# Query heads prepared inside the first projection, keys and the rest left to the heads stage

## The chip, the core and the metric

The kernel runs on one core of a Trainium2 chip. The metric is the device time of one launch in microseconds (us). The engines are named as in the profile: PE (TensorE), DVE (VectorE), ACT (ScalarE), POOL (GpSimd), and SP, whose queue issues most transfers.

## What is computed

A two-layer model over 2048 latent and 256 context tokens (2304 in all, 18 tiles of 128), width 1024. Only the first half of layer 0 matters here:

```
h  = layer_norm(x) * (1 + scale) + shift          # scale, shift = silu(c) @ ada_w + ada_b
q, ga, k, v, u, gb = split(h @ w_in)               # q: 12 heads of 64; k, v: 4 heads; u: 4 groups of 64
q  = rope(rms_norm(q, q_gain));  k = rope(rms_norm(k, k_gain))
y  = [attention(q, k, v) * silu(ga), fourier(rms_norm(u, f_gain)) * silu(gb)] @ w_out
```

Layer 1 (an mLSTM mixer) and the rest of layer 0 are the same in both kernels. float32 products are made of three passes over parts: every operand is split into a high part and the rest (low part), and `split_mm` issues high x high, high x low and low x high.

## The kernel before

The program is a row of stages with a barrier between them: `modulation`, `projections` (layer 0), `heads`, attention, and so on. Engines meet only by semaphores; each engine runs its own instructions in the order written.

**projections(0)** computes proj0 = h @ w0, 2560 columns in NCH = 5 chunks of 512, token tile after token tile: 90 steps k = (c, t), 24 matmuls each. During chunk 0 each tile is also normalised and transposed (8 PE transposes through the PSUM tile `tp`). Step k needs the high and low parts of its tile, made by ACT (`high`, L374) and DVE (`low`, L479) into a ring of RING = 4 slots, two steps ahead from chunk 1 on. The result lands in one of NACC = 3 accumulators; ACT empties it in chunks 0, 3 and 4 (L398), DVE in chunks 1 and 2 (L490), into a ring of three stages that SP stores to DRAM (L329). So step k waits for the eviction of step k-3, and slot reuse makes `high(k+2)` wait for an older step. The weights of the next chunk come in two pieces of 1 MB: ACT loads and rounds them (L358), POOL subtracts (`low_w`, L433).

**heads** then reads proj0 back, tile by tile (ring of four tiles, 1536 columns each). ACT squares 20 groups of 64 (12 query heads, 4 key heads, 4 Fourier groups) with 20 instructions (L684); POOL makes the rotation table (L719) and the inverse norms (L728, L730, a power over 20 values); DVE multiplies by the table (L764), adds the halves (L772, L773), scales (L781 queries, L782 keys, L790 Fourier rows); PE transposes six pairs of query heads (L830) and four of keys (L837); ACT copies the high parts out (L693, L695), DVE the low parts (L798, L800). SP stores the queries of a tile with four transfers of 192 KB made of 512-byte pieces (L640). Keys stay in SBUF in `kres`. In the same stage run the `hm_` steps, the modulation vectors of the later stages: 16 pieces of `ada_w`, 1 MB each, one per tile, in nbuf = 2 buffers. At n == 4, SP also fills a constant part of `kres` (eight transfers, L665) and loads all values into `vres` (L666).

Of the kernel before, what the change touches and what calls it, by code (L numbers as in the profile page):

```python
# [20 lines left out]
F32 = mybir.dt.float32  # L21
# [5 lines left out]
P = 128  # L27
# [4 lines left out]
NT = T // P  # L32
# [206 lines left out]

def projections(nc, m, a, s, keep, layer):  # L240
# [11 lines left out]
    K, RING, NST, NACC, PIECES, NX = len(steps), 4, 3, 3, 2, 3  # L252
# [20 lines left out]
    if not L0:  # L273
# [6 lines left out]
        sg_done, sgz_done = m.sem(tag + "sg_done"), m.sem(tag + "sgz_done")  # L280
    x_ld, stats_done, var_done, rstd_done, xn_done = m.sem(tag + "x_ld", NX), m.sem(tag + "stats_d"), m.sem(tag + "var"), m.sem(tag + "rstd_d"), m.sem(tag + "xn")
# [21 lines left out]
    with nc.Block() as block:  # L303

        @block.sync
        def _(sp):
# [5 lines left out]
            for n in range(NX):  # L312
                load_x(n)
            for k, (c, t) in enumerate(steps):
# [22 lines left out]
        def _(act):  # L337
# [79 lines left out]
        def _(pool):  # L417
# [24 lines left out]
            for j in range(3, PIECES * NCH):  # L442
                low_w(j)

        @block.vector
        def _(dve):
# [50 lines left out]

            statistics(0)
# [23 lines left out]
        def _(pe):  # L522
# [72 lines left out]
def heads(nc, m, a, s, keep, kres, vres):  # L595

    NHD, NU, NR_RAW = NQ + NKV, FW // HD, 4
    NS, ND, NPAIR = NHD + NU, NQ + 2 * NKV, NQ // 2
    SPLIT = ((0, NQ), (NQ, NHD))
    raw = m.sb("hd_raw", [P, NR_RAW, C_GATE])  # L600
    rope = m.sb("hd_rope", [P, NR_RAW, 2, 32])
    table = m.sb("hd_table", [P, 2, 2, 4, 32])
# [1592 lines left out]
```

## Time and profile before

| what | value |
|---|---|
| median of 3 runs (lowest, highest) | 3894.47 us (3892.74, 3899.06) |
| profiled execution: its time, its span | 3897.25 us, 3895.6 us |
| busy share of the span: PE, DVE, ACT, POOL | 91%, 56%, 34%, 38% |
| projection 0, first x load to last step | about 38 to 580 us |
| heads stage, its first transfer to the first of the next stage | 583.88 to 761.28 us |
| mean granted PE clock, whole span | 0.942 |

The profile is one execution; the span is from the first to the last instruction. The two stages touched are 18% of it. PE is near full in the projection and about half idle in heads, so the shares of the whole span say little of either: each has to be read by itself.

### The profile page before, as it was taken

The page shows a single profiled execution, that of the slowest core. Times are in us where ns is not written, and L with a number is a line of the kernel's source. Part 1 is how long each engine was busy: PE and PEld are TensorE (multiplying, and loading weights), DVE is VectorE, ACT ScalarE, POOL GpSimd, SP SyncE. Part 2 cuts the span into 40 slices and gives each one's busy share as a digit, 9 for nine tenths or more (in the row PEclk, how much of TensorE's full clock was granted, in tenths as well). Part 3 has the DMA queues.
Part 4 walks back from the last instruction along what each step waited for, and adds up shares of the span by engine and source line. Part 5 has one row for each costly group of instructions (what it writes and reads, how often), then busy time and mean ns, then how long its engine had stood idle before and what let it go on. Part 6 is the DMA issues. An engine that isn't in the chain of part 4 may idle for free. (4 is left out here: it accounts for less than half of the span.)

```text
span 3895.6 us, 51321 instructions
## 1 busy us (share of the span) xinstructions
PE 3558.3 (91%) x17340; PEld 2683.5 (69%) x17340; DVE 2176.2 (56%) x3411; ACT 1315.6 (34%) x2466; POOL 1466.9 (38%) x937
## 2 busy tenths in 40 slices
PE   6999994689999999999959969999999995999798
PEld 4788872356666666666558857888998884887586
DVE  4633217856676666666536655333334443777576
ACT  2422326524444444444320034222223331664300
POOL 1100006627767776777713321000000101444354
PEclk8999995589999999999979979999999997999899
DMA  5321219811111111111065433212211112768553
GB/s 187 102 71 60 71 49 308 264 32 38 36 33 33 35 39 32 33 33 40 16 207 168 144 125 102 71 71 71 68 64 46 45 36 91 229 210 252 207 202 142
DMA packets 310817, 396.02 MB, mean 102 GB/s; under 512 B 79100, under 2 KB 207500, under 8 KB 310496
## 3 DMA queue, kind: packets, MB, share of 16 engines
q1 hardware_dynamic: 278304, 319.08, 26.2%
q10 hardware_dynamic: 21184, 37.46, 3.1%
q0 software_dynamic: 11136, 36.98, 2.4%
q8 instruction: 113, 1.85, 0.2%
q14 instruction: 80, 0.66, 0.1%
HBM read 269.76 MB, written 121.20 MB: 100 GB/s over the span
## 5 line engine op out<-in xcount | busy, mean ns | idle before, releaser
L1042 DVE TENSOR_REDUCE al_mx<-al_sx 128x1 f32<-128x512 f32 (+1 forms) x960 | 562.2, 631 | 268.9 <-PE al_sx L1119 255.4
L235 PE MATMUL pj_acc<-pj_whi,pj_h_hi 128*128 128x512 f32 x1808 | 709.9, 393 | 0.0
L236 PE MATMUL pj_acc<-pj_wlo,pj_h_hi 128*128 128x512 f32 x1808 | 706.0, 390 | 0.0
L237 PE MATMUL pj_acc<-pj_whi,pj_h_lo 128*128 128x512 f32 x1808 | 705.3, 390 | 0.0
L982 ACT ACTIVATE al_e<-al_st 128x1024 f32<-128x1024 f32 x432 | 442.6, 1025 | 578.1 <-PE al_st L1132 567.2
L479 DVE TENSOR_TENSOR pj_h_lo<-pj_hall,pj_h_hi 128x1024 fp32r<-128x1024 f32 x258 | 376.9, 1462 | 259.4 <-ACT pj_h_hi L374 259.3
L433 POOL TENSOR_TENSOR pj_wlo<-pj_wst,pj_whi 128x2048 fp32r<-128x2048 f32 x28 | 128.8, 4601 | 955.2 <-ACT pj_whi L358 955.2
L1012 POOL TENSOR_TENSOR al_acc_p<-al_acc_p,al_e 128x1024 f32<-128x1024 f32 x192 | 456.6, 2378 | 20.0 <-POOL al_acc_p L1012 0.4
L374 ACT ACTIVATE pj_h_hi<-pj_hall 128x1024 fp32r<-128x1024 f32 x258 | 270.8, 1056 | 530.8 <-PE pj_acc L237 513.4
L1141 PE MATMUL al_acc<-al_e,vres 128*64 128x512 f32 x1728 | 402.6, 601 | 0.0
L237 PEld LDWEIGHTS pj_acc<-pj_whi,pj_h_lo 128*128 128x128 f32 x1808 | 340.9, 189 | 71.9
L235 PEld LDWEIGHTS pj_acc<-pj_whi,pj_h_hi 128*128 128x128 f32 x1808 | 341.4, 189 | 70.4 <-issue 0.6
L236 PEld LDWEIGHTS pj_acc<-pj_wlo,pj_h_hi 128*128 128x128 f32 x1808 | 341.3, 189 | 69.5
L1131 PE MATMUL al_st<-al_qa,kres 128*128 128x512 f32 x864 | 344.9, 399 | 3.7 <-DMA al_qb<-al_negm 3.3
L1132 PE MATMUL al_st<-al_qb,kres 128*128 128x512 f32 x864 | 340.4, 394 | 0.0
L490 DVE COPY pj_stage<-pj_acc 128x512 f32<-128x512 f32 x122 | 84.3, 691 | 417.1 <-PE pj_acc L237 417.1
L1119 PE MATMUL al_sx<-kres,al_qx 128*128 128x512 f32 (+1 forms) x960 | 298.6, 394 | 9.6 <-DMA al_qx<-s_q 7.2
L1119 PEld LDWEIGHTS al_sx<-kres,al_qx 128*128 128x128 f32 x960 | 172.0, 191 | 158.6 <-issue 121.8
L1008 POOL TENSOR_TENSOR al_acc_p<-al_e 128x1024 f32<-128x1024 f32 x48 | 160.3, 3340 | 307.6 <-ACT al_e L982 307.6
L1141 PEld LDWEIGHTS al_acc<-al_e,vres 128*64 128x64 f32 x1728 | 111.2, 136 | 211.2 <-issue 194.8
L235 PE MATMUL mo_acc<-ow_whi,mo_y_hi 128*128 128x512 f32 x544 | 216.1, 397 | 0.0
L237 PE MATMUL mo_acc<-ow_whi,mo_y_lo 128*128 128x512 f32 x544 | 213.1, 392 | 0.0
(282 smaller groups left out, 5777.7 us busy)
## 6 DMA issues: line engine op xcount, KB each, us to landing
s_proj<-pj_stage SPq DMA_DIRECT2D x162, 256.0 KB, 2.0
pj_wst<-in_w ACTq DMA_DIRECT2D x28, 1024.0 KB, 5.7
ml_k<-s_proj SPq DMA_DIRECT2D x36, 512.0 KB, 4.4
ml_v<-s_proj SPq DMA_DIRECT2D x36, 512.0 KB, 8.7
mo_in<-s_proj SPq DMA_DIRECT2D x34, 512.0 KB, 6.0
hm_w<-in_ada_w SPq DMA_DIRECT2D x16, 1024.0 KB, 8.5
ml_qt<-s_qt SPq DMA_DIRECT2D x32, 512.0 KB, 6.1
s_h<-ml_h POOLq DMA_DIRECT2D x32, 512.0 KB, 8.0
```

The lines of the kernel that those rows point to most:

```text
L235: nc.tensor.matmul(out, s_hi, m_hi, start=start, stop=False)
L236: nc.tensor.matmul(out, s_hi, m_lo, start=False, stop=False)
L237: return nc.tensor.matmul(out, s_lo, m_hi, start=False, stop=stop)
L374: nc.scalar.activation(h_hi[:, k % RING], hall[:, :, t, :], ACT.Copy).then_inc(hi_done, 1)
L479: V.tensor_tensor(h_lo[:, k % RING], hall[:, :, t, :], h_hi[:, k % RING].bitcast(F32), ALU.subtract).then_inc(lo_done, 1)
L982: nc.scalar.activation(e[:, pair(p, j), :, :], st[(NP * p + j) % 2][:, :, 0:W], ACT.Exp).then_inc(e_done, 1)
L1012: nc.gpsimd.tensor_tensor(acc_p[:], acc_p[:], e[:, pair(p, j)], ALU.add).then_inc(add_p, 1)
L1042: V.tensor_reduce(mx[:, x:x + 1], slots[x % NSX][:, 0:spans[x % NS][1]], AX.X, ALU.max).then_inc(sx_max, 1)
L1119: mm(slots[x % NSX][:, 0:width], qx[:, p, i * P:(i + 1) * P], kres[:, g, lo:lo + width], start=True, stop=True).then_inc(sx_mm, 1)
L1131: mm(dst[:, t, 0:W], kres[:, g, keys], qa[:, p, :], start=True, stop=False)
L1132: y = mm(dst[:, t, 0:W], kres[:, NKV + g, keys], qb[:, p, :], start=False, stop=True)
L1141: y = mm(acc[t * HD:(t + 1) * HD, 0:W], vres[:, 2 * j + t, g, :], e[:, pair(p, j), t, :], start=(j == 0), stop=(j == NP - 1))
```

## The change

The twelve query heads leave `heads`. A new class `QueryHeads` does their work inside `projections(0)`, spread over the steps of chunks 1 to 4: tile n starts at step START + 3n = 21 + 3n, one tile every three steps. `due(k, after)` gives the tile whose piece with that offset falls on step k: SP reads 768 columns back at -2; ACT squares and POOL makes the table at -1; DVE sums and multiplies and POOL makes the norms at 0; DVE turns at 1 and scales at 2; PE transposes and ACT copies the high parts at 4; DVE subtracts at 5; SP stores at 6. The x buffers of chunk 0 and the PSUM tile `tp0` are used again for it. RING goes from 4 to 3 in layer 0. POOL's `low_w` calls are written at steps 5 and 12 of a chunk instead of ahead of everything.

`heads` keeps keys, Fourier rows and modulation: it loads 768 columns instead of 1536, makes 8 squares instead of 20 and norms over 8 values; `vres` is filled by an ACT copy per tile instead of one transfer; the key transposes alternate between two PSUM tiles; the `ada_w` pieces have four buffers and four are loaded ahead; the query stores are gone.

```diff
+    def load(self, sp, t):
+        if t >= 3:
+            sp.wait_ge(self.sq_done, t - 2)
+            sp.wait_ge(self.px_done, t - 2)
+            sp.wait_ge(self.table_done, t - 2)
+        sp.dma_start(self.x[:, t % 3, 0:QW], self.s["proj0"][t * P:(t + 1) * P, 0:QW]).then_inc(self.ld[t % 3], 16)
+        sp.dma_start(self.rope[:, t % 3], self.a["rope"][t * P:(t + 1) * P]).then_inc(self.ld[t % 3], 16)
...
+    def store(self, sp, t):
+        sp.wait_ge(self.hi_done, t + 1)
+        sp.wait_ge(self.lo_done, t + 1)
+        pairs = self.s["q"].rearrange("(i e) (w d) n -> e w d i n", e=2, w=2)
+        for e in range(2):
+            for w, part in enumerate((self.hi, self.lo)):
+                sp.dma_start(pairs[e, w, :, :, t * P:(t + 1) * P],
+                             part[e * HD:(e + 1) * HD].rearrange("p b i n -> p (b i) n").bitcast(F32)).then_inc(self.stored, 16)
+
+    def squares(self, act, t):
+        self.loaded(act, t)
+        if t:
+            act.wait_ge(self.ss_done, t)
+        self.nc.scalar.activation(self.sq, self.x[:, t % 3, 0:QW].rearrange("p (s h d) -> p s h d", s=3, d=HD), ACT.Square).then_inc(self.sq_done, 1)
...
+    def high(self, act, t):
+        act.wait_ge(self.tr_done, t + 1)
+        if t:
+            act.wait_ge(self.lo_done, t)
+            act.wait_ge(self.stored, 64 * t)
+        self.nc.scalar.activation(self.hi[:], self.tq, ACT.Copy).then_inc(self.hi_done, 1)
...
+        self.nc.gpsimd.tensor_tensor(self.table[:].rearrange("p c (i d) -> p c i d", i=2), self.rope[:, t % 3].unsqueeze(2).broadcast_to([P, 2, 2, 32]),
+                                     self.gain[:].rearrange("p (i d) -> p i d", i=2).unsqueeze(1).broadcast_to([P, 2, 2, 32]), ALU.mult).then_inc(self.table_done, 1)
+
+    def norms(self, pool, t):
+        p = t % 2
+        pool.wait_ge(self.ss_done, t + 1)
...
+        self.nc.gpsimd.tensor_tensor(self.rs[:, p], self.ss[:, p], self.eps[:], ALU.add).then_inc(self.eps_done, 1)
+        pool.wait_ge(self.eps_done, t + 1)
+        self.nc.gpsimd.tensor_tensor(self.rs[:, p], self.rs[:, p], self.power[:], ALU.pow).then_inc(self.rs_done, 1)
...
+    def sums(self, dve, t):
+        dve.wait_ge(self.sq_done, t + 1)
+        if t >= 2:
+            dve.wait_ge(self.rs_done, t - 1)
+        self.nc.vector.tensor_reduce(self.ss[:, t % 2].rearrange("p (s h) -> p s h", s=3), self.sq, AX.X, ALU.add).then_inc(self.ss_done, 1)
+
+    def products(self, dve, t):
+        dve.wait_ge(self.table_done, t + 1)
+        if t:
+            dve.wait_ge(self.turn_done, 2 * t)
+        self.nc.vector.tensor_tensor(self.px[:], self.raw(t).unsqueeze(1).broadcast_to([P, 2, NQ, HD]),
+                                     self.table[:].unsqueeze(2).broadcast_to([P, 2, NQ, HD]), ALU.mult).then_inc(self.px_done, 1)
...
+    def turned(self, dve, t):
+        dve.wait_ge(self.px_done, t + 1)
+        if t:
+            dve.wait_ge(self.tr_done, t)
+        V, px, turn = self.nc.vector, self.px, self.turn
+        V.tensor_tensor(turn[:, :, 0:32], px[:, 0, :, 0:32], px[:, 1, :, 32:64], ALU.subtract).then_inc(self.turn_done, 1)
+        V.tensor_tensor(turn[:, :, 32:64], px[:, 0, :, 32:64], px[:, 1, :, 0:32], ALU.add).then_inc(self.turn_done, 1)
+
+    def scaled(self, dve, t):
+        dve.wait_ge(self.turn_done, 2 * t + 2)
+        dve.wait_ge(self.rs_done, t + 1)
+        self.nc.vector.tensor_tensor(self.turn[:], self.turn[:], self.rs[:, t % 2].unsqueeze(2).broadcast_to([P, NQ, HD]), ALU.mult).then_inc(self.rot_done, 1)
+
+    def low(self, dve, t):
+        dve.wait_ge(self.hi_done, t + 1)
+        if t:
+            dve.wait_ge(self.stored, 64 * t)
+        self.nc.vector.tensor_tensor(self.lo[:], self.tq, self.hi[:].bitcast(F32), ALU.subtract).then_inc(self.lo_done, 1)
...
+    def transposes(self, pe, t, ident):
+        pe.wait_ge(self.rot_done, t + 1)
+        if t:
+            pe.wait_ge(self.hi_done, t)
+            pe.wait_ge(self.lo_done, t)
+        for i in range(NQ // 2):
+            x = self.nc.tensor.transpose(self.tq[:, i // self.half, i % self.half, :], self.turn[:, 2 * i:2 * i + 2, :].rearrange("p h d -> p (h d)"), ident)
+        x.then_inc(self.tr_done, 1)
...
-    K, RING, NST, NACC, PIECES, NX = len(steps), 4, 3, 3, 2, 3
+    K, RING, NST, NACC, PIECES, NX = len(steps), 3 if L0 else 4, 3, 3, 2, 3
...
+    START, EVERY = NT + 3, 3
+    due = lambda k, after: (k - START - after) // EVERY if L0 and (k - START - after) % EVERY == 0 and 0 <= k - START - after < EVERY * NT else None
...
+                n = due(k, -2)
+                if n is not None:
+                    for i in (n, NT + n):
+                        sp.wait_ge(stored[i % NST], 16 * (i // NST) + 16)
+                    if n == 0:
+                        sp.wait_ge(tr_done, NT)
+                    hq.load(sp, n)
+                n = due(k, 6)
+                if n is not None:
+                    hq.store(sp, n)
+            if L0:
+                sp.wait_ge(hq.stored, 64 * NT)
...
+                n = due(k, -1)
+                if n is not None:
+                    if n == 0:
+                        act.wait_ge(tr_done, NT)
+                    hq.squares(act, n)
+                n = due(k, 4)
+                if n is not None:
+                    hq.high(act, n)
...
-            for j in range(3, PIECES * NCH):
-                low_w(j)
+            low_w(3)
+            for k, (c, t) in enumerate(steps):
+                if c and c + 1 < NCH and k - first_of[c] in (5, 12):
+                    low_w(PIECES * (c + 1) + (k - first_of[c]) // 12)
+                n = due(k, -1)
+                if n is not None:
+                    hq.tables(pool, n)
+                n = due(k, 0)
+                if n is not None:
+                    hq.norms(pool, n)
...
+                n = due(k, 0)
+                if n is not None:
+                    hq.sums(dve, n)
+                    hq.products(dve, n)
+                n = due(k, 1)
+                if n is not None:
+                    hq.turned(dve, n)
+                n = due(k, 2)
+                if n is not None:
+                    hq.scaled(dve, n)
+                n = due(k, 5)
+                if n is not None:
+                    hq.low(dve, n)
...
+                n = due(k, 4)
+                if n is not None:
+                    if n == 0:
+                        pe.wait_ge(hf_dve, NT)
+                        pe.wait_ge(hf_act, NT)
+                    hq.transposes(pe, n, keep["ident"][:])
...
-    mod = Modulation(nc, m, "hm_", a, s, [(0, 4), (0, 5)] + [(1, c) for c in range(6)], 2, 1)
+    mod = Modulation(nc, m, "hm_", a, s, [(0, 4), (0, 5)] + [(1, c) for c in range(6)], 4, 1)
...
-                sp.dma_start(raw[:, n % NR_RAW, :], s["proj0"][n * P:(n + 1) * P, 0:C_GATE]).then_inc(ld[n % NR_RAW], 16)
+                sp.dma_start(raw[:, n % NR_RAW, :], s["proj0"][n * P:(n + 1) * P, QW:C_GATE]).then_inc(ld[n % NR_RAW], 16)
...
-            mod.load(sp, 0)
+            for n in range(NR_RAW):
+                if n:
+                    load(n)
+                mod.load(sp, n)
             for n in range(NT):
-                if n + 1 < PIECES:
-                    mod.load(sp, n + 1)
-                if n:
-                    store(n - 1)
                 if n + NR_RAW < NT:
                     sp.wait_ge(sq_done, n + 1)
...
                     load(n + NR_RAW)
+                if n + NR_RAW < PIECES:
+                    mod.load(sp, n + NR_RAW)
...
-                    sp.dma_start(vres[:, :, :, 0:HD].rearrange("p t h d -> p t (h d)"), s["proj0"][:, C_V:C_U].rearrange("(t p) n -> p t n", p=P)).then_inc(v_ld, 16)
-            store(NT - 1)
...
+                nc.scalar.activation(vres[:, n].rearrange("p h d -> p (h d)"), r[:, V_AT:U_AT], ACT.Copy)
                 for i in range(NS):
-                    at = i * HD if i < NHD else C_U + (i - NHD) * HD
+                    at = i * HD if i < NKV else U_AT + (i - NKV) * HD
                     x = nc.scalar.activation(sq[:, i, :], r[:, at:at + HD], ACT.Square, accum_out=ss[:, n % 2, i:i + 1])
...
-            low_parts(NT - 1)
+                if n:
+                    low_part(n - 1)
+            low_part(NT - 1)
...
-                pe.wait_ge(rot_done, 2 * n + 1)
+                pe.wait_ge(rot_done, n + 1)
                 if n >= 2:
-                    pe.wait_ge(qlo_done, n - 1)
-                    pe.wait_ge(qhi_done, n - 1)
...
+                    pe.wait_ge(klo_done, n - 1)
+                    pe.wait_ge(khi_done, n - 1)
```

How the rows move. First DVE in chunk 1 (`pj0_h_lo` is the low part of a tile, `pj0_stage` the eviction of an accumulator). Before, two instructions alternate:

```order
L490 COPY pj0_stage<-pj0_acc0 128x512
L479 TENSOR_TENSOR pj0_h_lo<-pj0_hall,pj0_h_hi 128x1024
L490 COPY pj0_stage<-pj0_acc1 128x512
L479 TENSOR_TENSOR pj0_h_lo<-pj0_hall,pj0_h_hi 128x1024
L490 COPY pj0_stage<-pj0_acc2 128x512
```

The same place of the changed kernel, three steps:

```order
L637 TENSOR_TENSOR pj0_h_lo<-pj0_hall,pj0_h_hi 128x1024
L326 TENSOR_REDUCE hq_ss<-pj0_x 128x12
L332 TENSOR_TENSOR hq_px<-pj0_x,hq_table 128x1536
L648 COPY pj0_stage<-pj0_acc0 128x512
L637 TENSOR_TENSOR pj0_h_lo<-pj0_hall,pj0_h_hi 128x1024
L340 TENSOR_TENSOR hq_turn<-hq_px 128x12x32
L341 TENSOR_TENSOR hq_turn<-hq_px 128x12x32
L648 COPY pj0_stage<-pj0_acc1 128x512
L637 TENSOR_TENSOR pj0_h_lo<-pj0_hall,pj0_h_hi 128x1024
L346 TENSOR_TENSOR hq_turn<-hq_turn,hq_rs 128x768
L352 TENSOR_TENSOR hq_lo<-pj0_tp0,hq_hi 128x768
L648 COPY pj0_stage<-pj0_acc2 128x512
```

Six instructions of the query work now stand between the evictions and low parts of three steps. Next SP's queue in `heads`, six rows of one tile of the kernel before (`hm_w` is a piece of `ada_w`; two more query stores stand ahead of them):

```order
L640 DMA s_q<-hd_qhi 64x6x128
L640 DMA s_q<-hd_qlo 64x6x128
L631 DMA hd_raw<-s_proj 128x1536
L632 DMA hd_rope<-in_rope 128x64
L122 DMA hm_w<-in_ada_w 128x4x512
L127 DMA hm_bias<-in_ada_b 1x512
```

and SP's queue of the changed kernel, three steps of the projection (waits as the semaphores' names, partly names of earlier owners):

```order
L459 DMA s_proj0<-pj0_stage 128x512 [waits pj0_out]
L270 DMA pj0_x<-s_proj0 128x768 [waits mod_mm,mod_ld7,mod_ld6,pj0_stored0]
L271 DMA hq_rope<-in_rope 128x64
L459 DMA s_proj0<-pj0_stage 128x512 [waits pj0_out] x2
L282 DMA s_q<-hq_hi 64x6x128 [waits mod_stored,mod_row_out]
L282 DMA s_q<-hq_lo 64x6x128
```

The four query stores (two more follow the last row shown) left the heads queue and stand behind the third step's store; in `heads` a tile keeps the L631, L632 and L122 rows, the first at half its width.

## Rows read from the trace of the kernel before

**Rows 1.** Windows: length; busy PE, PEld, DVE, ACT, POOL; PE clock; DMA share; GB/s

```profile
194.00:580.00 386.00, 385.81 (x1703) 319.24 (x1701) 118.91 (x105) 100.08 (x110) 27.65 (x6) 1.00 0.18 63
583.90:761.30 177.40, 97.27 (x364) 47.97 (x364) 142.82 (x226) 116.52 (x769) 120.06 (x73) 0.56 0.94 300
583.90:590.00 6.10, 0.00 (x0) 0.00 (x0) 2.14 (x4) 0.00 (x0) 0.00 (x0) 0.50 0.68 203
640.00:650.00 10.00, 4.98 (x24) 2.15 (x18) 8.65 (x15) 7.82 (x51) 7.48 (x5) 0.67 1.03 244
690.00:710.00 20.00, 13.88 (x56) 6.49 (x54) 19.90 (x30) 17.35 (x111) 18.50 (x12) 0.59 1.05 376
```

**Rows 2.** Transfers of the heads stage, 583 to 762 us, median us to landing

```profile
DMA packets 47024, 53.30 MB, mean 298 GB/s; under 512 B 5200, under 2 KB 35408, under 8 KB 47008
...
hm_w<-in_ada_w SPq DMA_DIRECT2D x16, 1024.0 KB, 8.5
hd_raw<-s_proj SPq DMA_DIRECT2D x18, 768.0 KB, 6.2
s_q<-hd_qhi SPq DMA_DIRECT2D x36, 192.0 KB, 6.5
```

**Rows 3.** Groups of the heads stage, mean ns of one, idle before

```profile
L684 ACT ACTIVATE hd_sq<-hd_raw 128x64 f32<-128x64 f32 x360 | 86.2, 242 | 14.9 <-DMA hd_rope<-in_rope 13.2 <-POOL hd_rs L730 1.5
L730 POOL TENSOR_TENSOR hd_rs<-hd_rs,hd_half 128x20 f32<-128x20 f32 x18 | 68.3, 3796 | 1.4
...
L764 DVE TENSOR_TENSOR hd_px<-hd_raw,hd_table 128x1536 f32<-128x1536 f32 x18 | 31.4, 1744 | 0.9 <-POOL hd_table L719 0.9
L719 POOL TENSOR_TENSOR hd_table<-hd_rope,hd_g 128x256 f32<-128x256 f32 x18 | 30.9, 1719 | 129.2 <-DVE hd_g L804 128.7
L830 PE MATMUL hd_tq<-keep_ident,hd_rot 128*128 128x128 f32 x108 | 27.7, 429 | 62.5 <-DVE hd_rot L781 62.5
...
L772 DVE TENSOR_TENSOR hd_turn<-hd_px 128x512 f32<-128x512 f32 x18 | 18.6, 1033 | 0.6
...
L781 DVE TENSOR_TENSOR hd_rot<-hd_turn,hd_rs 128x768 f32<-128x768 f32 x18 | 17.3, 963 | 3.8 <-POOL hd_rs L730 3.8
L798 DVE TENSOR_TENSOR hd_qlo<-hd_tq,hd_qhi 128x768 fp32r<-128x768 f32 x18 | 17.1, 949 | 19.0 <-ACT hd_qhi L693 18.9
```

**Rows 4.** SP's queue in order of time: start, us, transfers issued

```profile
580.47 0.33 SPq L329 DMA_DIRECT2D s_proj<-pj_stage  x1
583.88 0.34 SPq L631 DMA_DIRECT2D hd_raw<-s_proj  x1
...
638.47 10.10 SPq L665 DMA_DIRECT2D kres<-hd_rows  x8
...
754.23 0.59 SPq L640 DMA_DIRECT2D s_q<-hd_qhi  x1
...
761.28 0.34 SPq L913 DMA_DIRECT2D ac_fold<-in_fold  x1
```

**Rows 5.** PE in chunk 0: eight transposes, then the next step

```profile
152.20 1.09 PE L529 MATMUL pj_tp<-keep_ident,pj_x 128*128 128x128 f32 x8 [0.35 <-DVE pj_x L464]
153.04 0.47 PE L235 MATMUL pj_acc<-pj_whi,pj_h_hi 128*128 128x512 f32 x1
```

**Rows 6.** Groups of projection 0 from 194 to 583 us

```profile
L374 ACT ACTIVATE pj_h_hi<-pj_hall 128x1024 fp32r<-128x1024 f32 x68 | 71.9, 1058 | 143.7 <-PE pj_acc L237 143.7
L433 POOL TENSOR_TENSOR pj_wlo<-pj_wst,pj_whi 128x2048 fp32r<-128x2048 f32 x6 | 27.7, 4608 | 265.8 <-ACT pj_whi L358 265.8
L490 DVE COPY pj_stage<-pj_acc 128x512 f32<-128x512 f32 x36 | 24.9, 691 | 122.0 <-PE pj_acc L237 122.0
...
L358 ACT ACTIVATE pj_whi<-pj_wst 128x2048 fp32r<-128x2048 f32 x6 | 11.4, 1902 | 0.0
```

**Rows 7.** Low parts in the same window, ns min/median/max of one

```profile
L479 DVE TENSOR_TENSOR pj_h_lo<-pj_hall,pj_h_hi x69: 1211/1224/4867, 194.2 to 565.1; 128x1024 fp32r<-128x1024 f32 x69
```

**Rows 8.** Transfers of the projection, 194 to 583 us, us to landing

```profile
s_proj<-pj_stage SPq DMA_DIRECT2D x72, 256.0 KB, 2.0
```

More of the change, by code:

```diff
@@ L237, in split_mm, with __init__, raw, load_gain @@
     return nc.tensor.matmul(out, s_lo, m_hi, start=False, stop=stop)
+class QueryHeads:
+    def __init__(self, nc, m, a, s, x, tp):
+        self.nc, self.a, self.s, self.x = nc, a, s, x
+        self.half = NQ // 4
+        self.tq = tp[:, :, 0:self.half * P].rearrange("p b (i n) -> p b i n", n=P)
+        self.sq = x[:, :, QW:].rearrange("p s (h d) -> p s h d", d=HD)
+        self.rope, self.table = m.sb("hq_rope", [P, 3, 2, 32]), m.sb("hq_table", [P, 2, HD])
+        self.gain = m.sb("hq_gain", [P, HD])
+        self.ss, self.rs = m.sb("hq_ss", [P, 2, NQ]), m.sb("hq_rs", [P, 2, NQ])
+        self.eps, self.power = m.sb("hq_eps", [P, NQ]), m.sb("hq_power", [P, NQ])
+        self.px, self.turn = m.sb("hq_px", [P, 2, NQ, HD]), m.sb("hq_turn", [P, NQ, HD])
+        self.hi, self.lo = m.sb("hq_hi", [P, 2, self.half, P], F32R), m.sb("hq_lo", [P, 2, self.half, P], F32R)
+        self.gain_ld, self.ld, self.stored = m.sem("hq_gain_ld"), m.sem("hq_ld", 3), m.sem("hq_stored")
+        self.const, self.table_done, self.sq_done, self.ss_done = (m.sem("hq_" + n) for n in ("const", "table", "sq", "ss"))
+        self.eps_done, self.rs_done, self.px_done, self.turn_done = (m.sem("hq_" + n) for n in ("eps_d", "rs_d", "px_d", "turn_d"))
+        self.rot_done, self.tr_done, self.hi_done, self.lo_done = (m.sem("hq_" + n) for n in ("rot_d", "tr", "hi_d", "lo_d"))
+    def raw(self, t):
+        return self.x[:, t % 3, 0:QW].rearrange("p (h d) -> p h d", d=HD)
+    def load_gain(self, eng):
+        eng.dma_start(self.gain[:], self.a["qk_gain"][:, 0:HD].broadcast_to([P, HD])).then_inc(self.gain_ld, 16)
+    def load(self, sp, t):
[5 more added lines that the diff above has]
+        sp.dma_start(self.rope[:, t % 3], self.a["rope"][t * P:(t + 1) * P]).then_inc(self.ld[t % 3], 16)
+    def loaded(self, eng, t):
+        eng.wait_ge(self.ld[t % 3], 32 * (t // 3) + 32)
+    def store(self, sp, t):
[17 more added lines that the diff above has]
+        self.nc.scalar.activation(self.hi[:], self.tq, ACT.Copy).then_inc(self.hi_done, 1)
+    def constants(self, dve):
+        self.nc.vector.memset(self.eps[:], HD * EPS).then_inc(self.const, 1)
+        self.nc.vector.memset(self.power[:], -0.5).then_inc(self.const, 1)
+    def tables(self, pool, t):
+        self.loaded(pool, t)
+        if t == 0:
+            pool.wait_ge(self.gain_ld, 16)
+        else:
+            pool.wait_ge(self.px_done, t)
+        self.nc.gpsimd.tensor_tensor(self.table[:].rearrange("p c (i d) -> p c i d", i=2), self.rope[:, t % 3].unsqueeze(2).broadcast_to([P, 2, 2, 32]),
[3 more added lines that the diff above has]
+        pool.wait_ge(self.ss_done, t + 1)
+        if t == 0:
+            pool.wait_ge(self.const, 2)
+        if t >= 2:
+            pool.wait_ge(self.rot_done, t - 1)
+        self.nc.gpsimd.tensor_tensor(self.rs[:, p], self.ss[:, p], self.eps[:], ALU.add).then_inc(self.eps_done, 1)
[3 more added lines that the diff above has]
+        dve.wait_ge(self.sq_done, t + 1)
+        if t >= 2:
+            dve.wait_ge(self.rs_done, t - 1)
[30 more added lines that the diff above has]
+        x.then_inc(self.tr_done, 1)
@@ L313, in _ @@
                 load_x(n)
+            if L0:
+                hq.load_gain(sp)
             for k, (c, t) in enumerate(steps):
@@ L595, in heads @@
 def heads(nc, m, a, s, keep, kres, vres):
[L597 to L600, printed above, removed]
+    NU, NR_RAW = FW // HD, 4
+    NS = NKV + NU
+    WIDE = C_GATE - QW
+    V_AT, U_AT = C_V - QW, C_U - QW
+    raw = m.sb("hd_raw", [P, NR_RAW, WIDE])
     rope = m.sb("hd_rope", [P, NR_RAW, 2, 32])
-    table = m.sb("hd_table", [P, 2, 2, 4, 32])
+    table = m.sb("hd_table", [P, 2, 2, HD])
     sq = m.sb("hd_sq", [P, NS, HD])
@@ L824, in _ @@
                 p = n % 2
[L825 removed]
+                pe.wait_ge(rot_done, n + 1)
                 if n >= 2:
[L827 to L835 removed]
+                    pe.wait_ge(klo_done, n - 1)
+                    pe.wait_ge(khi_done, n - 1)
                 for i in range(NKV):
[L837 removed]
+                    tr = nc.tensor.transpose(four(tk[p])[:, i, :], rot[:, p, i].rearrange("p e d -> p (e d)"), keep["ident"][:])
                 tr.then_inc(tk_done, 1)
```

111 lines of the change are left out of this document (36 added, 75 removed).

## The prediction

> **What bounds the kernel now.** I read the windows first, because the change touches two stages and the shares of the span mix them with the rest. In the later chunks of the projection [rows 1] PE is busy 385.81 of 386.00 us at the full clock (1.00, the 2.4 GHz level), while DVE is busy 119 us, ACT 100 and POOL 28, with the transfer engines at 0.18. PE alone bounds it. 1703 matmuls at 24 a step are 71 steps, so a step takes 386/71 = 5.44 us. The groups [rows 6] say the same from the other side: what DVE and ACT wait for is PE.
>
> In heads the window [rows 1] shows 177.4 us with DVE busy 142.8, POOL 120, ACT 117, PE 97 (clock 0.56, mostly the 1.2 GHz level), but the transfer engines at 0.94. In the steady stretch 690 to 710 us two things are full at once: DVE, 19.90 of 20, and the transfers, 1.05 at 376 GB/s. Taking work from DVE alone would leave the transfers as the bound; the change takes from both. There is also a hole: the low parts of the queries (L798) were preceded by 19.0 us of DVE idle time [rows 3]. It follows SP's eight fills of `kres`, whose issue alone took 10.10 us [rows 4]. The chain that ended last says little on heads, so I don't use it.
>
> **Heads, by bytes.** The stage moved 53.30 MB [rows 2]. Gone are the query stores, 72 of 192 KB = 14.2 MB; half of every tile read, 18 of 384 KB = 7.1 MB; and the load of `vres`, 2.4 MB. 29.7 MB stay, 16.8 of them `ada_w`. The opening moves 1.2 MB in 6.1 us (203 GB/s), the `kres` fills 2.4 MB at the 244 GB/s of their window, 9.7 us, and the other 26.1 MB at 376 GB/s take 69.4 us [rows 1]. That makes 85.2 us of transfers.
>
> **Heads, by engines**, per tile. DVE: of 142.8 us go the query products 31.4, the scaling 17.3, the low parts 17.1 and three quarters of the turns (L772 18.6 and its twin L773, taken alike: 28), leaving 49/18 = 2.7 us. ACT: 12 x 18 squares at 0.242 = 52 us and some 12 of copies go, some 7 for `vres` come: 59/18 = 3.3. POOL: the power covers 8 values instead of 20; in proportion 3.8 us becomes 1.5 (nothing shorter than 20 is among my rows, so 1.5 to 3.8), 41 us less; the table halves, 15 less: 64/18 = 3.6, at most 5.8. PE: less 27.7 us of transposes, 70/18 = 3.9 at the same low clock [rows 1, 3]. Transfers: 0.43 + 1.05 + 0.13 MB = 1.6 MB, 4.3 us. So transfers bound a tile at 4.3 us where it was 7.9, and the engines come close behind.
>
> **The stage.** SP reads tile 17 only when tile 13 is used up, so when the transfers are through about four tiles remain, 4 x 4.1 = 16 us, of which about 3 overlap. The end was set by query stores: SP's queue shows the first of the last four at 754.23 and the next stage at 761.28 [rows 4]. What remains is the last store of Fourier rows and the barrier; from 580.47 to 583.88, less a landing of 2.0 [rows 8], a barrier costs 1.4, so I take 5.5 us. 85.2 + 16 - 3 + 5.5 = 103.7, I say 104 us: **73.4 us saved**. The bounds are 92 (transfers, then only the ending) and 126 (5.8 us a tile on POOL, 18 x 5.8 = 104, with 6 for the opening, 10 for the fills and 5.5 for the ending).
>
> **Projection, on PE.** 18 x 6 transposes come into a stage with no idle PE. Eight take 153.04 - 152.20 = 0.84 us [rows 5], six 0.63: **11.3 us added**, certain. In heads they cost 27.7 us but lay beside the bound, so that is no gain.
>
> **Projection, on the others.** Three steps now take 3 x 5.44 + 0.63 = 16.95 us. DVE has in them three low parts 3.7, three evictions 2.1, sums 0.95 (as L781, same size), products 1.74, turns 2 x 0.78 (three quarters of 1.03), scaling 0.96 and low parts 0.95: 11.9 of 16.95. ACT and POOL have more room. The evictions and `high`/`low` hide all this: `high(k+2)` and `low(k+2)` end 1.06 + 1.22 = 2.3 us after step k-1 [rows 6, 7] and are due two steps after it, a reserve of 8.6 us. RING = 3 only ties `high(k+2)` to the end of step k-1, inside that figure, so I cost it at nothing; if it hid worse, 0 to 1 us a step.
>
> What could go wrong is a ring of waits. ACT's copy of high parts waits for the stores of the tile before, which SP issued one step earlier, behind an eviction. Store issue and landing: 754.23 to 761.28 less 1.4 is 5.65 us [rows 4], upper bound for a quiet stretch. The ring: SP's own store 0.4, stores 5.65, copy 0.8 (three quarters of L374), `high` 1.06, then on DVE low part 1.22, scaling 0.96, query low parts 0.95, eviction 0.69, low part 1.22, sums 0.95, products 1.74, eviction 0.69 = 16.3 us, then SP again. That is 0.6 under 16.95, so the ring does not bind, but barely. Six times POOL's `low_w` (4.61 us) and ACT's rounding (1.90) come into it; a low part beside it took up to 4.87 instead of 1.22 [rows 6, 7]. Four of these fall in chunks 1 and 2, where DVE is in the ring: 4 x (3.65 + 1.90) = 22 us, less 11 tiles x 0.6 recovered, less the reserve 8.6 = 7 at most, 0 at least. I take **3 us**. In chunks 3 and 4 ACT evicts and the ring is shorter.
>
> A rule weighed against this. The rows: a low part that met `low_w` ended with it (4.87 against a median of 1.22), yet scaling in heads, beside a power that fills 3.8 of each 7.9 us, averaged 0.96 [rows 3, 7]. The Trainium skill, "SBUF — State Buffer", section "Who interferes with whom", has it that VectorE's two-input tensor_tensor from SBUF and GpSimd's reads exclude each other for a whole instruction. By that rule every new POOL instruction, the power too, would hold DVE; by the rows only the long subtraction does.
>
> **Sum.** -73.4 + 11.3 + 3 = -59.1 us on the span: 3836.5. The profiled execution took 3897.25 us, 2.8 over the median of the runs; 3897.25 - 59.1 = 3838.2, and from the median 3894.47 - 59.1 = **3835.4 us**.
>
> **Rivals.**
> - *Query stores land slower in the projection.* In heads one took 6.5 us [rows 2]; after three issues of 0.6 that is 8.3 instead of 5.65. Ring 18.95, 2.0 over, times 17 tiles less 8.6 = 25 us in place of my 3: 3858. For it: the same 512-byte pieces. Against: the transfer engines are at 0.18 there, and step stores land in 2.0 [rows 8]. 0.17, with anything from 5 to 40.
> - *POOL's new instructions hold DVE.* Power 2.3 (3.8 x 12/20), table 0.9 and addition 0.3 put into the ring: 19.8, 2.85 over, 40 us in place of 3: 3872. Against it the 0.96 above. 0.06. This is the rule of the page "SBUF — State Buffer" of the Trainium skill.
> - *Heads keeps its hole.* If the fills starve it again by some 20 us, though four tiles (16 us) are ahead: 3855. 0.13.
> - *Heads runs at its lower bound* of 92 us, buffers always ahead: 3823. 0.13.
> - *Slower than before.* The stores of one tile need longer than the ring's limit. The loss passes the 62 us left when (L - 16.95) x 17 - 8.6 = 62, L = 21.1, stores of 10.5 us instead of 5.65. With 12.5 (about twice that row) L = 23.1, +96: 3928. Nothing in a stretch at 0.18 points to it. 0.04.
> - *The forecast*: 0.47; its own range 3825 to 3850.
>
> **Range and chances.** 3812 to 3870 takes in both bounds of heads nearly whole (92 and 126 us give 3823 and 3857) and the stores' rival; outside stay the slower case, most of POOL's hold, and tails. A difference within 0.2% (8 us) can't be told from none. All cases but one lie more than that below: faster 0.95, same 0.01, slower 0.04.
>
> **What would show it.** Right: PE at 0.99 of the window of chunks 1 to 4 with steps of 5.44 and a tile's transposes 0.63; heads near 104 us, with DVE about half idle and tiles 4 to 4.5 us apart; next stages unchanged. Wrong: PE waiting for `pj_h_lo` or an eviction by DVE (the ring); ACT's high-part copy waiting for `s_q` until after the next step's end; DVE products beside POOL's power two or three times 1.74; in heads transfers well below 1.0 while every engine waits (a chain, not bytes).

## The result, and the profile after

The changed kernel took 3847.78 us (median of 4 runs, 3844.78 to 3853.84) against 3896.76 us (4 runs) of the kernel before: a ratio of 0.9873 with a 95% interval of 0.9857 to 0.9889, 49 us or 1.3% less. The forecast was 3835.4, with 3812 to 3870 as the range and 3825 to 3850 as the range of the likeliest case. Both hold the time, 12 us above the forecast.

The profiled execution's span went from 3895.6 to 3843.2 us. Where the 52.4 us come from is read off SP's queue, at the first transfer of each stage (start in us, time of issue, transfers):

```profile
601.63 0.33 SPq L459 DMA_DIRECT2D s_proj<-pj_stage  x1
605.12 0.34 SPq L807 DMA_DIRECT2D hd_raw<-s_proj  x1
...
706.08 0.33 SPq L1053 DMA_DIRECT2D ac_fold<-in_fold  x1
```

Heads starts at 605.12 instead of 583.88 [rows 4], 21.2 later. It lasts 101.0 instead of 177.4 us, 76.4 less. The rest of the program, whose code is the same, takes 3137.1 instead of 3134.3 us, 2.8 more; in the twelve profiled executions of this document it took 3131.3 to 3137.1, so this is scatter. 21.2 - 76.4 + 2.8 = -52.4.

Windows of the changed kernel (length; busy PE, PEld, DVE, ACT, POOL; PE clock; transfer share; GB/s), the projection and then heads:

```profile
194.00:590.00 396.00, 388.19 (x1757) 320.81 (x1756) 221.44 (x212) 124.33 (x143) 118.28 (x60) 1.00 0.42 117
605.10:706.10 101.00, 60.73 (x256) 20.09 (x256) 66.16 (x172) 56.82 (x337) 57.66 (x73) 0.67 0.86 293
611.00:631.00 20.00, 11.66 (x41) 2.98 (x42) 11.98 (x34) 11.73 (x79) 12.28 (x16) 0.59 1.04 387
646.00:656.00 10.00, 7.06 (x32) 3.34 (x24) 5.78 (x17) 1.55 (x11) 3.98 (x5) 0.66 1.00 233
686.00:696.00 10.00, 8.17 (x28) 1.98 (x28) 7.08 (x20) 6.81 (x41) 6.47 (x9) 0.61 0.40 148
696.00:706.00 10.00, 2.39 (x10) 0.93 (x10) 6.11 (x20) 3.62 (x14) 3.34 (x5) 0.73 0.11 40
```

Two readings. In the projection PE is no longer full: 388.19 of 396 us, where it had been 385.81 of 386 [rows 1]. In heads no engine is near full (DVE 66 of 101 us), while the transfers run at 387 GB/s with a share of 1.04 for as long as there is something to read, and lie idle in the last 20 us.

What PE waits for in the projection, and what stands behind it (who waited for whom, us in all, times, longest):

```profile
DVE pj_h_lo L637 <- ACT pj_h_hi L516: 157.0, 43, 7.6
ACT hq_hi L296 <- DMA s_q<-hq_lo: 148.1, 17, 14.2
...
PE pj_tp L360 <- DVE hq_lo L352: 7.8, 4, 3.6
```

Step by step back: PE's query transposes wait for DVE's low part of the tile before (L352), DVE waits for ACT, and ACT sits 148 us before its copy of the high parts (L296), for the query stores. This is the ring of the prediction. One quiet turn of it, SP's queue:

```profile
264.28 0.60 SPq L282 DMA_DIRECT2D s_q<-hq_hi  x1
...
281.23 0.60 SPq L282 DMA_DIRECT2D s_q<-hq_hi  x1
```

ACT in the same stretch of the changed kernel (start, duration, line, operation, and in brackets the wait before it):

```profile
270.88 0.81 ACT L296 ACTIVATE hq_hi<-pj_tp 128x768 fp32r<-128x768 f32 x1 [10.97 <-DMA s_q<-hq_lo]
...
288.08 0.81 ACT L296 ACTIVATE hq_hi<-pj_tp 128x768 fp32r<-128x768 f32 x1 [11.18 <-DMA s_q<-hq_lo]
```

From the first store's issue to the copy pass 6.60 us, and 6.85 in the next turn; a turn, from copy to copy, takes 288.08 - 270.88 = 17.2 us. A turn with a subtraction of weights (`low_w`) in it is longer. POOL in one of them:

```profile
328.26 4.61 POOL L583 TENSOR_TENSOR pj_wlo<-pj_wst,pj_whi 128x2048 fp32r<-128x2048 f32 x1 [10.09 <-ACT pj_whi L500]
```

DVE beside it, a low part that takes 1.21 us elsewhere and here ends 1.1 us after the subtraction:

```profile
329.09 4.86 DVE L637 TENSOR_TENSOR pj_h_lo<-pj_hall,pj_h_hi 128x1024 fp32r<-128x1024 f32 x1
```

ACT around it, from copy to copy:

```profile
323.76 0.81 ACT L296 ACTIVATE hq_hi<-pj_tp 128x768 fp32r<-128x768 f32 x1 [12.13 <-DMA s_q<-hq_lo]
326.21 1.90 ACT L500 ACTIVATE pj_whi<-pj_wst 128x2048 fp32r<-128x2048 f32 x1
344.26 0.81 ACT L296 ACTIVATE hq_hi<-pj_tp 128x768 fp32r<-128x768 f32 x1 [14.23 <-DMA s_q<-hq_lo]
```

And DVE behind the second copy:

```profile
346.05 1.23 DVE L637 TENSOR_TENSOR pj_h_lo<-pj_hall,pj_h_hi 128x1024 fp32r<-128x1024 f32 x1 [6.30 <-ACT pj_h_hi L516]
347.19 1.21 DVE L346 TENSOR_TENSOR hq_turn<-hq_turn,hq_rs 128x768 f32<-128x768 f32 x1
348.33 0.94 DVE L352 TENSOR_TENSOR hq_lo<-pj_tp,hq_hi 128x768 fp32r<-128x768 f32 x1
```

From copy to copy 20.5 us instead of 17.2. PE at the end of this turn:

```profile
345.48 0.39 PE L237 MATMUL pj_acc<-pj_whi,pj_h_lo 128*128 128x512 f32 x1
349.42 1.51 PE L360 MATMUL pj_tp<-keep_ident,hq_turn 128*128 128x128 f32 x6 [3.56 <-DVE hq_lo L352]
350.59 0.78 PE L235 MATMUL pj_acc<-pj_whi,pj_h_hi 128*128 128x512 f32 x1
```

The transposes start 0.15 us after L352 ends at 349.27, 3.56 us after PE had run dry.

The turns add up to what PE lost. Eight of them, from the copy at 250.36 to that at 399.82, took 149.5 us, where PE needs 17.0 for three steps and six transposes, 135.9 in all: 13.5 us too much. Four took 17.1 to 17.3, three with a subtraction 20.5, 20.5 and 21.3, and one 18.4; in that one a query store took 2.26 us to issue instead of about 0.64, and why stays open. PE starts its transposes 5.17 us after such a copy when it has to wait; after the copy at 250.36 they were due only 8.2 us later (258.57), a reserve of 3.0. 13.5 - 3.0 = 10.5 us, the 10.5 that the first run below gives back. On PE itself 10.3 of them can be seen: about 8.8 us of gaps before the transposes (7.8 in the list of waits, the rest without a named releaser) and 1.5 at the lower clock behind the longest gap.

### The profile page after: what moved, and what is told of

Same layout as the page of the kernel before. It is cut to its first block and busy times, and to the rows that moved or that the text cites. A ratio compares the mean times of both kernels' runs of the same rounds, so it can differ in the third digit from the quotient of the medians.

```text
span 3843.2 us, 51226 instructions
## 1 busy us (share of the span) xinstructions
PE 3536.2 (92%) x17340; PEld 2668.7 (69%) x17340; DVE 2201.5 (57%) x3467; ACT 1281.6 (33%) x2070; POOL 1495.5 (39%) x991
## 5 line engine op out<-in xcount | busy, mean ns | idle before, releaser
L1281 PE MATMUL al_acc<-al_e,vres 128*64 128x512 f32 x1728 | 402.5, 601 | 0.0
```

Source lines behind the costliest of these rows:

```text
L1281: y = mm(acc[t * HD:(t + 1) * HD, 0:W], vres[:, 2 * j + t, g, :], e[:, pair(p, j), t, :], start=(j == 0), stop=(j == NP - 1))
```

## The experiments

Two measures come from each trace. For the projection: from DVE's first eviction of chunk 1 (192.10 in the changed kernel) to the first transfer of heads, which leaves out chunk 0, whose end scatters by up to 5 us from run to run. It is 390.3 us before and 413.0 after. For heads: from its first transfer to the first of the next stage.

Times without "(one)" are medians of several executions, those with it single ones; projection and heads are read from one profiled execution of each kernel.

| kernel | projection, us | heads, us | time, us |
|---|---|---|---|
| before | 390.3 | 177.4 | 3896.8 |
| changed | 413.0 | 101.0 | 3847.8 |
| e1_store_early | 402.5 | 104.7 | 3839.2 |
| e2_short_low_w | 402.5 | 104.2 | 3837.0 (one) |
| e3_before_ring3 | 390.3 | 175.3 | 3890.5 (one) |
| e4_one_transpose | 409.1 | 105.9 | 3846.0 (one) |
| e10_stores_twice | 456.0 | 103.4 | 3888.1 (one) |
| e5_full_width | 412.1 | 115.9 | 3859.8 (one) |
| e8_dve_twice | 412.4 | 105.6 | 3852.9 (one) |
| e7_two_buffers | 412.3 | 108.8 | 3849.0 (one) |
| e6_fills_late | 412.1 | 94.3 | 3833.2 |
| e9_both | 402.5 | 93.9 | 3826.0 |

The projection's measure repeats within 1 us. The same heads code gave 101.0, 104.7, 104.2, 105.9 and 103.4 us, mean 103.8, so a time between 101.0 and 105.9 is not read as an effect, and 103.8 is what the others are held against.

**The ring, shortened by order alone.** SP stores a tile's query parts one eviction earlier:

```diff
+                n = due(k, 6)
+                if n is not None:
+                    hq.store(sp, n)
                 evicted(sp, k)
...
                     hq.load(sp, n)
-                n = due(k, 6)
-                if n is not None:
-                    hq.store(sp, n)
```

> The changed kernel, with SP storing a tile's query parts before it waits for the eviction of that step, not after. Theory (ring of waits through the query stores): the copy of the high parts, which waited 148 us in all for the stores, waits a few us; PE's 7.8 us of waiting before the query transposes goes to 0 to 1 us, the projection ends 8 to 9 us earlier (last step store at about 593 instead of 602), heads unchanged at 101 us. Rival 1 (DVE simply has too much to do, or is held by POOL): PE's wait stays at 6 to 9 us, the total within 3 us of the changed kernel. Rival 2 (the wait is for DVE's own low part behind late ACT rounding of weights): the wait halves.

Measured: the projection's measure fell by 10.5 us, to 402.5, a little more than the 8 to 9 expected; the ratio to the kernel before is 0.9854 (0.9837 to 0.9870, four executions), which by itself overlaps that of the changed kernel. Heads did not stay at 101, but within its scatter. The waits of the projection in this kernel:

```profile
ACT hq_hi L296 <- DMA s_q<-hq_lo: 13.9, 13, 4.2
```

148.1 us of waiting became 13.9, and PE waits for nothing. Same instructions, same DVE and POOL work: rival 1 falls, and rival 2, by which half of the wait would have stayed, with it.

**The subtraction of weights, cut short.** Pieces 4 to 9 subtract 64 of 2048 values per partition:

```diff
-                nc.gpsimd.tensor_tensor(wlo[:, c % 2, part, :], wst[:], whi[:, c % 2, part, :].bitcast(F32), ALU.subtract).then_inc(w_lo, 1)
+                sub = slice(0, 1) if L0 and j > 3 else slice(0, KP)
+                nc.gpsimd.tensor_tensor(wlo[:, c % 2, part, :][:, sub, 0:64 if L0 and j > 3 else CH], wst[:, sub, 0:64 if L0 and j > 3 else CH], whi[:, c % 2, part, :][:, sub, 0:64 if L0 and j > 3 else CH].bitcast(F32), ALU.subtract).then_inc(w_lo, 1)
```

> The changed kernel, with POOL's subtraction for weight pieces 4 to 9 of layer 0 cut to 64 columns of one of four rows (most of the low parts of these weights are left out). If the 4.6 us subtractions beside DVE push the ring over PE's reserve: PE's wait before the query transposes goes from 7.8 us to under 1.5, the stage 6 to 8 us shorter. If the ring of stores alone is too long: the wait stays above 5 us, since nothing of the ring is POOL's.

The waits of the projection in this kernel:

```profile
ACT hq_hi L296 <- DMA s_q<-hq_lo: 113.8, 17, 10.0
```

The stores are still waited for, 113.8 us, and yet PE's stalls are gone: 402.5, exactly as in e1. The turn that took 20.5 us takes 17.3 here (321.38 to 338.67). So neither cause is enough: the ring alone (17.2 against 17.0 of PE) eats the reserve slowly, the subtractions push it over. Shortening either one frees PE. The same sum holds here: eight turns, from 251.60 to 390.43, took 138.8 us, 2.9 over PE's 135.9, with a reserve of 3.4 (transposes at 260.17, 8.6 after the first of these copies, less 5.17). One of the eight took 20.0 us without any subtraction; in it ACT's squares waited 4.7 us for the tile's loads, issued 0.3 to 1 us behind a weight piece of 1 MB. The edit lets the next weight piece load some us earlier, which this run doesn't separate.

**The ring, lengthened.** Every query part is stored twice, to a second tensor, and the copy waits for both:

```diff
-        pairs = self.s["q"].rearrange("(i e) (w d) n -> e w d i n", e=2, w=2)
-        for e in range(2):
+        both = [self.s[name].rearrange("(i e) (w d) n -> e w d i n", e=2, w=2) for name in ("q", "q2")]
+        for e, pairs in ((0, both[0]), (1, both[0]), (0, both[1]), (1, both[1])):
...
-            act.wait_ge(self.stored, 64 * t)
+            act.wait_ge(self.stored, 128 * t)
```

> The changed kernel, whose query parts are stored a second time to another place in DRAM, behind the first four stores of each tile, the copy of high parts waiting for all eight. Theory (ring): four more issues of 0.65 us and 0.8 MB more to land make the ring 2.6 to 4 us longer in each of the 17 turns, all of it on PE once the reserve is gone, also in chunks 3 and 4: 35 to 65 us more than the changed kernel in the projection, PE waiting before the query transposes. Rival (the stores are not on any path that binds, the waits came from DVE beside POOL): under 10 us more.

The same waits with the doubled stores:

```profile
ACT hq_hi L296 <- DMA s_q<-hq_lo: 217.7, 17, 18.4
...
PE pj_tp L360 <- DVE hq_lo L352: 38.6, 14, 7.4
```

43 us more than the changed kernel in the projection, inside what was expected, and nearly the whole gain of the change (3888.1, against 3892.1 for the kernel before measured with it, one execution each). One turn went from 411.16 to 432.06 on ACT, 20.9 us, 3.7 more than a quiet one of the changed kernel; the four further issues of a tile take that long (589.81 to 593.47 on SP). So stores for which PE never waits directly, in a stage whose transfer share was 0.42, cost PE what they add to the ring once it binds. Whether it is their issue or their landing that adds it, this run doesn't separate.

**Three slots instead of four, in the kernel before.**

```diff
-    K, RING, NST, NACC, PIECES, NX = len(steps), 4, 3, 3, 2, 3
+    K, RING, NST, NACC, PIECES, NX = len(steps), 3 if L0 else 4, 3, 3, 2, 3
```

> The kernel before with three slots instead of four for the high and low parts in layer 0 and nothing else changed. Costed at nothing: steps in chunks 1 to 4 stay at 5.44 us, the heads stage starts at 583.9 us give or take 0.5. Rival: the ring of three binds, and each step grows by 0.1 to 1 us, the stage by 7 us or more.

390.27 us, to the hundredth as before. In the kernel before it costs nothing. (Heads started at 582.36, 1.5 us earlier and so outside the half microsecond expected, all of it from chunk 0.)

**One transpose instead of six.**

```diff
-        for i in range(NQ // 2):
+        for i in range(1):
```

> The changed kernel with one query transpose per tile instead of six (most queries are left out). Theory: 90 transposes of 0.105 us go, 9.4 us, but PE's waits for the ring grow by what PE no longer fills: in chunks 1 and 2 the ring takes about 17.2 us per three steps against 16.4 of PE, so 11 x 0.8 less what the reserve holds, up to 9 us, comes back. The stage ends 2 to 9 us earlier than 602; in chunks 3 and 4 three steps take 16.4 instead of 17.0. Rival (transposes cost nothing): nothing changes in chunks 3 and 4.

3.9 us less, and where it arose tells more: the 36 evictions by ACT in chunks 3 and 4 took 192.1 us instead of 196.3 (from DVE's last to ACT's last), those by DVE in chunks 1 and 2 212.9 instead of 212.7. Where the ring binds, taking PE work away gives nothing back; where it doesn't, it gives all.

**Heads: more bytes, same instructions.** Reads of 1536 columns, 768 of them unused:

```diff
-    WIDE = C_GATE - QW
-    V_AT, U_AT = C_V - QW, C_U - QW
+    WIDE = C_GATE
+    V_AT, U_AT = C_V, C_U
...
-                sp.dma_start(raw[:, n % NR_RAW, :], s["proj0"][n * P:(n + 1) * P, QW:C_GATE]).then_inc(ld[n % NR_RAW], 16)
+                sp.dma_start(raw[:, n % NR_RAW, :], s["proj0"][n * P:(n + 1) * P, 0:C_GATE]).then_inc(ld[n % NR_RAW], 16)
```

> The changed kernel, whose heads stage reads 1536 columns of every tile again and uses 768 of them, as many instructions as before. The heads stage alone took 101.0 us in the changed kernel and 104.2 to 105.9 in three runs with the same heads code. Theory (bound by bytes while reads last): 7.1 MB more at about 380 GB/s are 18.6 us, so 119 to 124 us. Rival (bound by the chain of small instructions and waits from tile to tile): the reads hide, 101 to 108. The projection is untouched.

115.9 us, 12 over the mean: less than 18.6, clearly more than the chain's rival allows. By windows, transfers ran at a share of 1.04 and 398 GB/s in a steady stretch:

```profile
605.60:721.50 115.90, 68.80 (x256) 23.36 (x256) 65.45 (x172) 56.69 (x336) 54.68 (x72) 0.61 0.89 316
620.00:640.00 20.00, 13.98 (x53) 3.70 (x52) 12.21 (x32) 11.73 (x74) 11.99 (x16) 0.58 1.04 398
```

Two thirds of the added bytes show. That the rest hides because the first tiles and the end do not wait for reads is argued, not shown.

**Heads: more DVE work, same bytes.** The key products are made twice, first into a scratch tile:

```diff
+                V.tensor_tensor(px2[:], x.unsqueeze(1).broadcast_to([P, 2, NKV, HD]),
+                                table[:, p].unsqueeze(2).broadcast_to([P, 2, NKV, HD]), ALU.mult)
```

> The changed kernel, whose heads stage makes each tile's key products twice on DVE, 18 more instructions of 0.68 us, the first set into a scratch tile. Theory (bytes): the 12 us hide but for the last few tiles, heads 101 to 108 us. Rival (DVE or the tile's chain is the bound): 113 to 118.

The window of heads in this kernel:

```profile
609.00:714.60 105.60, 65.52 (x256) 22.01 (x256) 76.47 (x190) 56.83 (x337) 55.77 (x73) 0.62 0.85 280
```

DVE is busy 76.5 instead of 66.2 us, and heads takes 105.6, within the scatter and well under the 113 to 118 of the rival. Of the 10.3 us added on DVE 1.8 show over the mean, no more than the scatter; of 18.6 added in transfers, 12, well beyond it. Each is a single execution. While its reads last, heads is bound by bytes.

**Heads: two buffers for ada_w instead of four.**

```diff
-    mod = Modulation(nc, m, "hm_", a, s, [(0, 4), (0, 5)] + [(1, c) for c in range(6)], 4, 1)
+    mod = Modulation(nc, m, "hm_", a, s, [(0, 4), (0, 5)] + [(1, c) for c in range(6)], 2, 1)
...
-                mod.load(sp, n)
+                if n < 2:
+                    mod.load(sp, n)
...
-                if n + NR_RAW < PIECES:
-                    mod.load(sp, n + NR_RAW)
+                if 2 <= n + 2 < PIECES:
+                    mod.load(sp, n + 2)
```

> The changed kernel with two buffers for the pieces of ada_w, loaded two ahead, as in the kernel before. Theory (heads bound by bytes, deep buffers only cover the fills): 101 becomes 104 to 112 us, the hole at the fills grows. Rival (the queue depth is what made heads short): 120 us or more. Rival (depth is worth nothing): 100 to 102.

108.8 us, 5 over the mean, 2.9 over the highest of the five, and as expected: by this one execution depth is a small part of the 76 us.

**The fills of kres, late.**

```diff
-                if n == 4:
+                if n == 14:
                     sp.wait_ge(rows_done, 2)
```

> The changed kernel with the eight fills of kres issued after tile 13 is used up (n == 14) instead of at n == 4. Transfers are full at n == 4 and nearly idle at the end of heads (0.40 and 0.11 of the engines in the last 20 us). Theory (heads is bound by transfers until its last reads are in): the 2.4 MB, 9.7 us, move into the idle end, the hole of 10 us in DVE goes, and heads takes 92 to 96 us instead of 101. Rival (the tiles' own chain bounds it): under 2 us. Second rival: the fills then end last, and the stage is not shorter or longer by up to 3 us.

Windows of heads, and of its last 18 us:

```profile
603.80:698.10 94.30, 64.04 (x256) 21.82 (x256) 65.83 (x172) 57.07 (x336) 57.65 (x73) 0.65 0.93 314
...
680.00:690.00 10.00, 6.46 (x29) 1.51 (x28) 5.81 (x17) 7.44 (x40) 6.39 (x8) 0.86 0.94 214
690.00:698.00 8.00, 0.65 (x4) 0.42 (x4) 3.36 (x12) 0.99 (x2) 0.54 (x1) 0.69 0.11 38
```

94.3 us, 9.5 under the mean. The 2.4 MB moved from a stretch in which they displaced reads (646 to 656 us above: 233 GB/s, ACT busy 1.55 of 10) to one in which the transfers had lain idle (0.40 before, 0.94 now). Ratio 0.9847 (0.9826 to 0.9868).

**Early stores and late fills together.**

> Early stores and late fills together. The two touch different stages, so the gains add: 8 plus 6 us, some 14 us under the changed kernel, 3833 or so. Rival: the earlier end of the projection or the end of heads is then set by something else and the sum is 8 at most.

3825.97 us (4 runs), ratio 0.9816 (0.9800 to 0.9833), an interval that lies wholly under that of the changed kernel: 402.5 and 93.9 us, the two gains add. Its median is 70 us under the kernel before and 22 under the changed one.

## Why the prediction was right, and by how much not

- **Transposes, 11.3 us on PE.** Right in kind. Without stalls (e1, e2, e9) the measure is 402.5, 12.2 over before, or 0.68 per tile instead of 0.63. That the same work gave nothing in heads fits what was measured there, but no run takes out the transposes alone.
- **The ring, 3 us (0 to 7).** The mechanism was there and named; this term was mis-sized, and what it measured lies outside its own bounds: 413.0 - 402.5 = 10.5 us. Three figures in it were off. "Store issue and landing", 5.65 us, taken as the "upper bound for a quiet stretch", was 6.6 to 6.85. The quiet turn above splits into 5.02 us from the copy to the end of the query low part (4.99 in the prediction), 4.87 to DVE's second eviction after it (5.29), 0.46 for SP's own store (0.4) and 6.85 for the stores. So it took 17.2 us, not 16.3, and recovered nothing. At a tile's stores the projection's transfers are not quiet: a window from 340 to 342 us has a share of 0.99 at 217 GB/s. "The reserve 8.6" was that of the low parts of h; the first thing late is PE's transposes, which need DVE's query low part of the tile before. By the prediction's own terms that ends 11.0 us after the eviction and is due 16.26 after it, 5.2 us later, and at the copy of 250.36 there were 3.0 left. And a turn with a subtraction was 3.3 to 4.1 us longer (20.5 to 21.3 against 17.2), less than the 5.55 assumed, in three turns and not four: the first of the four subtractions, at 221.38, came before the first query store (243.79).
- **"Query stores land slower in the projection"** (0.17, "anything from 5 to 40") came half true. They took up to 6.85 us, between the forecast's 5.65 and this rival's 8.3, and the 10.5 us of the ring lie in its range. Its sign, ACT's copy waiting for `s_q` past the next steps, showed; PE waited for `hq_lo` and not, as also named, for `pj_h_lo` or an eviction.
- **RING = 3 at nothing.** Shown by e3 for the kernel before, and in the changed one the 12.2 us of transposes are all that stays without stalls.
- **POOL's hold on DVE.** The rival by which all new POOL work holds DVE would have made 3872. In a quiet turn DVE's product (278.42 to 280.16) took its 1.74 us beside POOL's addition, and it was the addition that grew, to 1.66 us against 0.20 for one over 8 values in heads. A low part of 1.21 us lay within POOL's power (280.31 to 282.58) and was not held at all. POOL's table product did hold DVE a little: a low part that began 0.04 us behind it took 1.51, so "only the long subtraction does" was not quite right. A turn stayed at 17.2. Where a product met a subtraction it took 5.59 us, as on DVE here in the changed kernel:

```profile
257.62 5.59 DVE L332 TENSOR_TENSOR hq_px<-pj_x,hq_table 128x1536 f32<-128x1536 f32 x1
```

The Trainium skill, "SBUF — State Buffer", section "Who interferes with whom", has a two-input instruction of DVE and GpSimd's reads exclude each other, the order of issue deciding who waits. The subtraction, the table product and the addition agree with it (5.59 for 1.74, 1.51 for 1.21, 1.66 for 0.20); the power, with no visible hold, does not.
- **Heads, 104 us, 73.4 saved.** Measured 101.0 in the profiled execution, 103.8 in the mean of five, so the 104 were met and the 3 us under it are scatter. Bytes as the bound is shown by e5 against e8. The bound of 5.8 us a tile on POOL was far off: the power over 8 values took 1.69 us, near the 1.5 in proportion.
- **"Heads keeps its hole"**, given 0.13 and 20 us, was half true: a hole of some 10 us stayed within the 104, and e6 took it out.
- **Slower than before** (0.04): e10 shows where that lay. With twice the stores nearly everything is gone.

The sum of what was off in the profiled execution: +7.5 in the ring, +0.9 in transposes, -3.0 in heads, +2.8 in stages not touched, and -1.5 from chunk 0: 6.7 us, the difference of 52.4 and 59.1. The 12.4 us by which the median missed hold 5.7 more, both of them scatter between executions: the forecast started from a median of before that lay 2.8 under its profiled execution (it moved from 3894.5 to 3896.8 with one more run), and the profiled execution of the changed kernel lies 2.9 under its own median. The -3.0 in heads and the +2.8 after it are scatter too and cancel, which is luck; the ring is the one error of substance.

What stays open: whether the earlier loading of weights in e2 has a part in its gain; no run held it fixed. Where the 12 of 18.6 us in e5 come from tile by tile was argued, not shown. How the 76 us of heads divide over the stores, the halved reads and the load of `vres` that left it was not tested piece by piece.

## What to carry to other kernels

When work moves beside a stage with one full engine, add up not only each engine's load but every ring of waits that the new work closes, transfers included, and compare it with the period of the full engine; its reserve is that of the earliest-due consumer, not of the one that was there before. A single buffer between a producer and a store puts the whole landing into such a ring, and the order of two lines in the issuing queue can take it out. A stage bound by bytes wants constants and other transfers that nobody waits for in its idle end.

## What the runs showed of the hardware

PE's pause of 3.56 us was followed by a lower clock: the window behind it has 0.50 of the granted clock, the 1.2 GHz level, where it was 1.00 before and 0.97 after. Behind the three shorter pauses (0.32, 1.19 and 2.71 us) the clock stayed at 1.00. Windows of the changed kernel, columns as above, the first of them the one cited for the stores, the last behind the pause of 2.71:

```profile
340.00:342.00 2.00, 2.00 (x10) 1.65 (x10) 0.00 (x0) 0.00 (x0) 0.00 (x0) 1.00 0.99 217
340.00:348.00 8.00, 5.87 (x26) 4.51 (x25) 1.95 (x2) 3.47 (x5) 1.26 (x1) 1.00 0.87 233
349.00:352.00 3.00, 2.58 (x9) 2.33 (x10) 3.00 (x5) 0.02 (x1) 0.05 (x1) 0.50 0.35 132
352.00:360.00 8.00, 8.00 (x36) 6.58 (x35) 4.90 (x6) 0.00 (x0) 3.87 (x2) 0.97 0.59 138
387.60:390.60 3.00, 2.85 (x16) 2.50 (x17) 3.00 (x5) 0.00 (x0) 0.32 (x1) 1.00 0.23 87
```

Behind the pause of 3.56 us the six transposes took 1.17 us to the next matmul instead of 0.60, and the next four matmuls 1.84 us instead of 0.91. From these transposes to the next tile's PE took 18.45 us instead of 16.99, 1.5 us on top of the pause, two fifths of its length.

In the stretches with query stores of 512-byte pieces the transfer engines were at 0.99 and moved 217 GB/s, against 387 at 1.04 in heads of the changed kernel, which has no such stores. The length of the pieces alone doesn't explain it: heads of the kernel before moved 376 GB/s at 1.05 [rows 1] with the same stores among its transfers. POOL's addition over 12 values took 1.64 us on average in the projection, beside DVE, where I had put 0.3; it hides.
